# One modulation block summed on VectorE, modulation products moved behind the last sums, and low parts in another order

## The reference

```python
# first block, layer i of 2 (i = 0: differential attention, i = 1: neighbourhood attention)
sh1, sc1, g1, sh2, sc2, g2 = split(silu(c) @ ada_w[i] + ada_b[i], 6)          # for x
csh1, csc1, cg1, csh2, csc2, cg2 = split(silu(c_ctx) @ ada_w[i] + ada_b[i], 6)  # for ctx
h = rmsnorm(x, norm_mix[i]) * (1 + sc1) + sh1      # and hc from xc with csc1, csh1
x = x + g1 * attention(h, hc)                      # q, k, v = h @ wqkv, then @ wo
h2 = rmsnorm(x, norm_ffn[i]) * (1 + sc2) + sh2
x = x + g2 * conv_ffn(h2, ffn_up[i], ffn_conv[i], ffn_conv_b[i], ffn_down[i])
# ctx gets the same FFN in layer 0 only

# second block, layer l of 2
proj = rmsnorm(x, norm_g[l]) @ w_in[l]             # NSA, pool, conv, FoX, gates, merge
kc = silu(blocks(k_c) @ cmp_w1[0] + cmp_b1[0]) @ cmp_w2[0] + cmp_b2[0]   # nsa_compress, vc alike
x = x + merged_branches @ w_out[l]
```

## Time and profile before

| | us |
|---|---|
| median of 3 runs | 1631.76 (1630.92 to 1633.79) |
| the profiled execution's own time | 1631.88 |
| its span | 1629.8 |
| PE busy | 1600.1 (98%) |
| DVE busy | 930.7 (57%) |
| ACT busy | 768.1 (47%) |
| POOL busy | 548.2 (34%) |

### The profile page before, as it was taken

How to read it: one execution, slowest core, us unless ns; L and a number is a source line. 1 busy time by engine, 2 the same in 40 slices (tenths; PEclk the granted TensorE clock), 3 DMA queues, 4 the chain that set the end, 5 groups by cost and what they waited for, 6 DMA issues and landing times.

```text
span 1629.8 us, 24693 instructions
## 1 busy us (share of the span) xinstructions
PE 1600.1 (98%) x9894; PEld 1347.8 (83%) x9894; DVE 930.7 (57%) x1477; ACT 768.1 (47%) x1410; POOL 548.2 (34%) x358
## 2 busy tenths in 40 slices
PE   8999999999999999999999999999999999999998
PEld 5778557778767888879767999999999989999987
DVE  4434585555423554342265888649775567568545
ACT  5323585534313433243274755445645455454554
POOL 2224243412201222222172111026434666423554
PEclk9999999999999999999999999999999999799999
DMA  9264600443255222365314654545435544433551
GB/s 394 78 251 180 228 6 27 181 170 133 86 183 191 103 80 71 123 214 173 103 27 165 253 180 158 176 174 183 154 130 182 181 158 167 155 130 130 181 192 67
DMA packets 52465, 249.27 MB, mean 153 GB/s; under 512 B 20608, under 2 KB 20736, under 8 KB 25856
## 3 DMA queue, kind: packets, MB, share of 16 engines
q1 hardware_dynamic: 43600, 243.90, 41.9%
q10 hardware_dynamic: 8752, 3.80, 0.9%
HBM read 246.63 MB, written 1.05 MB: 152 GB/s over the span
## 4 chain that ended last, share of the span: by engine, by line
PE 89%; DVE 6%; DMA 1%; ACT 1%; issue 1%; SPq 0%; POOL 0%; POOLq 0%; ACTq 0%; DVEq 0%
PE psq L547 14%; PE psq L549 14%; PE psq L548 14%; PE psq L931 7%; PE ps L547 6%; PE ps L549 6%; PE ps L548 6%; PE psq L932 4%; PE ps L931 3%; PE ps L561 2%; PE ps L932 1%; DVE WL L529 1%; PE psq L1340 1%; PE ps L1368 1%; PE psq L2250 1%
## 5 line engine op out<-in xcount | busy, mean ns | idle before, releaser
L529 POOL TENSOR_TENSOR WL<-RAW,WH 128x1024 fp32r<-128x1024 f32 (+2 forms) x116 | 303.8, 2621 | 537.1 <-ACT WH L519 525.9
L529 DVE TENSOR_TENSOR WL<-RAW,WH 128x1024 fp32r<-128x1024 f32 (+3 forms) x264 | 325.5, 1258 | 271.8 <-ACT WH L519 271.6
L519 ACT ACTIVATE WH<-RAW 128x1024 fp32r<-128x1024 f32 (+2 forms) x380 | 361.0, 1001 | 163.2 <-DMA RAW<-wstream 115.1
L547 PE MATMUL psq<-NHL,WH 128*128 128x256 f32 (+1 forms) x1264 | 412.9, 327 | 2.6 <-DVE NHL L834 1.6
L549 PE MATMUL psq<-NHL,WL 128*128 128x256 f32 (+1 forms) x1264 | 406.8, 322 | 0.0
L548 PE MATMUL psq<-NHL,WH 128*128 128x256 f32 (+1 forms) x1264 | 406.7, 322 | 0.0
L547 PEld LDWEIGHTS psq<-NHL,WH 128*128 128x128 f32 x1264 | 241.7, 191 | 31.6 <-issue 8.7
L549 PEld LDWEIGHTS psq<-NHL,WL 128*128 128x128 f32 x1264 | 241.6, 191 | 18.0
L548 PEld LDWEIGHTS psq<-NHL,WH 128*128 128x128 f32 x1264 | 241.8, 191 | 16.8
L931 PE MATMUL psq<-NHL,WH 128*128 128x512 f32 x416 | 148.6, 400 | 0.0
L547 PE MATMUL ps<-NHL,WH 128*128 128x256 f32 (+1 forms) x368 | 122.1, 332 | 0.0
(11 more groups left out here) (388 smaller groups left out, 2877.2 us busy)
## 6 DMA issues: line engine op xcount, KB each, us to landing
RAW<-wstream SPq DMA_DIRECT2D x196, 1024.0 KB, 4.9
RAW<-wstream SPq DMA_DIRECT2D x32, 704.0 KB, 4.1
K<-first SPq DMA_DIRECT2D x4, 1024.0 KB, 16.6
X<-xin SPq DMA_DIRECT2D x2, 1024.0 KB, 6.4
V<-first SPq DMA_DIRECT2D x2, 1024.0 KB, 19.4
Q<-first SPq DMA_DIRECT2D x2, 1024.0 KB, 24.9
BR<-rpb ACTq DMA_DIRECT2D x8, 256.0 KB, 7.8
BR<-rpb SPq DMA_DIRECT2D x8, 256.0 KB, 8.3
```

The source lines that it names most:

```text
L519: e.activation(WH[:, u % 3, a:z], RAW[:, v % 3, a:z], ACT.Copy).then_inc(w_hi, 1)
L529: e.tensor_tensor(WL[:, u % 3, a:z], RAW[:, v % 3, a:z], WH[:, u % 3, a:z].bitcast(F32), ALU.subtract).then_inc(w_lo_p if pool else w_lo_v, 1)
L547: e.matmul(o, lh, rh, start=start, stop=False)
```

## The change

There are five parts.

1. The eight modulation products of block 4 leave PE. DVE multiplies each unit by its column of silu(c), one number per partition, and adds it into a new tile WSUM, 128x2048 (`dve_ada_step`: one TENSOR_SCALAR, seven SCALAR_TENSOR_TENSOR), two steps in the first down product's turn, one in each of the next six, always ahead of that turn's low parts. SP waits for these steps where it waited for PE. One product of four matmuls with a stationary of ones (`pe_ada_joint`) sums WSUM over the partitions, ahead of the second product of the second half of up; ACT's copy of the bank follows there.
2. In passage 1, PE's modulation products with units 1 and 2 of block 3 stand behind the sums of tile 7 (unit 1) and behind the spreading of the root (unit 2) instead of between the sums and ahead of the spreading. In passage 2 only one product of block 5 instead of two stands between the last sums and the root's spreading; the fourth of the block goes ahead of qkv unit 5 of layer 1.
3. In passages 1 to 3 the first tile of the first unit starts with the four matmuls that need only its high part (`pe_high_first`); the two that need its low part follow.
4. ACT copies the row of block 3 one product earlier.
5. In the head of the second block, DVE writes the low part of cmp0 between the product and the sum of KN's rotation, no longer behind the sum.

```diff
-QKV_ADA = {("qkv", 1, 4): (0, 1, 2, 3)}
+QKV_ADA = {("qkv", 1, 4): (0, 1, 2), ("qkv", 1, 5): (3,)}
+JOINT_ADA = {("up", 0, HALF_FT + 1): (7,)}
...
     for m in range(DT):
-        run_ada(4, m)
         add(("down", 0, 0, m), 2)
         add_ada(4, m)
...
         def load_unit(e, v):
-            if v >= 3 and v - 3 not in SPLIT_AT:
+            if v >= 3 and KEYS[v - 3][:2] == ("ada", 4):
+                e.wait_ge(ada_acc, KEYS[v - 3][2] + 1)
+            elif v >= 3 and v - 3 not in SPLIT_AT:
                 e.wait_ge(gemm, product(KEYS[v - 3]))
...
+        def dve_ada_step(e, k):
+            v = UNIT_OF["ada", 4, k]
+            e.wait_ge(d_raw[v % 3], 16 * (v // 3 + 1))
+            if k == 0:
+                e.tensor_scalar(WSUM[:, :], RAW[:, v % 3, :], CB[:, k, 0:1], None, ALU.mult).then_inc(ada_acc, 1)
+                return
+            e.wait_ge(ada_acc, k)
+            e.scalar_tensor_tensor(out=WSUM[:, :], in0=RAW[:, v % 3, :], scalar=CB[:, k, 0:1], in1=WSUM[:, :],
+                                   op0=ALU.mult, op1=ALU.add).then_inc(ada_acc, 1)
+
+        def pe_ada_joint(e):
+            e.wait_ge(ada_par, 3)
+            e.wait_ge(ada_acc, 8)
+            for j in range(4):
+                mm = e.matmul(AB[32 * j:32 * j + 32, :], ONE.to_broadcast([P, 32]), WSUM[:, 512 * j:512 * j + 512],
+                              start=True, stop=True)
+            mm.then_inc(gemm, 1)
...
+        def pe_high_first(e, n, key, outs, T, shared):
+            v, wh, wl = weights(key)
+            wait_weights(e, v, 0)
+            e.wait_ge(n_hi, split_base(n) + NORM_T[n] // 256)
+            for j, o in enumerate(outs):
+                w = slice(P * j, P * j + P)
+                e.matmul(o, wh[:, 0, w], NH[:, 0, 0:T], start=j == 0 or not shared, stop=False, skip_group_check=shared)
+                e.matmul(o, wl[:, 0, w], NH[:, 0, 0:T], start=False, stop=False, skip_group_check=shared)
+            pe_wait_norm(e, n, 0)
+            for j, o in enumerate(outs):
+                e.matmul(o, wh[:, 0, P * j:P * j + P], NL[:, 0, 0:T], start=False, stop=False, skip_group_check=shared)
...
             pe_sums(e, n, 6)
-            if l == 0:
-                pe_ada(e, 3, 1)
             pe_sums(e, n, 7)
-            if l == 0:
-                pe_ada(e, 3, 2)
-            else:
-                pe_ada(e, 6, 1)
+            pe_ada(e, 6 if l else 3, 1)
...
+                    if l == 0 and c == 1 and jj == 1:
+                        pe_ada_joint(e)
...
         def pe_down(e, l, c):
             for m in range(DT):
-                if l == 0 and c == 0:
-                    pe_ada(e, 4, m)
...
                 pe_ada(e, 5, 1)
-                pe_ada(e, 5, 2)
...
-                    if l == 0 and c == 0 and jj == 8:
+                    if l == 0 and c == 0 and jj == 7:
                         act_ada_row(e, 3)
+                    if l == 0 and c == 1 and jj == 1:
+                        act_ada_row(e, 4)
...
                     for half in range(1 if l == 0 else 2):
+                        if l == 0 and c == 0 and m == 0:
+                            dve_ada_step(e, 0)
+                        if l == 0 and c == 0 and m < DT - 1:
+                            dve_ada_step(e, m + 1)
                         if not (last and half):
                             split_lo(e, ahead(key), False)
...
             e.memset(CM[:, 0:384].bitcast(U32), 0).then_inc(cm_zero, 1)
-            dve_turn(e, l, 1, KN[:, :, :])
+            dve_turn_product(e, l, 1)
             lo_prep(e, l, "kf", False)
+            dve_turn_sum(e, l, 1, KN[:, :, :])
```

More of the change, by code:

```diff
@@ L228, in unit_orders @@
             add(("out", l, i), 1)
-    for name, at, b in (("up", UP_ADA, 3), ("qkv", QKV_ADA, 5), ("up", LATE_ADA, 6)):
+    for name, at, b in (("up", UP_ADA, 3), ("qkv", QKV_ADA, 5), ("up", LATE_ADA, 6), ("up", JOINT_ADA, 4)):
         for key, ks in at.items():
@@ L399, in bass_two_block_decoder @@
             HL[0] = sb("HL0", [P, HALF_FT, 512], F32R, scope)
+            WSUM = sb("WSUM", [P, 2048], F32, scope)
         with ExitStack() as scope:
@@ L465, in bass_two_block_decoder @@
         c_silu, c_zero, lam_v, lam_exp = (sem(n) for n in ("c_silu", "c_zero", "lam_v", "lam_exp"))
-        ada_row, ada_fin, ada_half, ada_par, amod = (sem(n) for n in ("ada_row", "ada_fin", "ada_half", "ada_par", "amod"))
+        ada_row, ada_fin, ada_half, ada_par, ada_acc, amod = (
+            sem(n) for n in ("ada_row", "ada_fin", "ada_half", "ada_par", "ada_acc", "amod"))
         x_res, x_low, x_sq, x_sq_v, sq_acc, sq_sum, g_pair = (
@@ L884, in pe_wide @@
             if abreast:
-                for k in range(nk):
+                for k in range(1, nk):
                     wait_weights(e, v, k)
@@ L889, in pe_wide @@
                         mm = mm3(e, o, wh[:, k, P * j:P * j + P], wl[:, k, P * j:P * j + P], xh[:, k, 0:T],
-                                 xl[:, k, 0:T], k == 0, k == nk - 1)
+                                 xl[:, k, 0:T], False, k == nk - 1)
                         if k == nk - 1:
@@ L943, in pe_both @@
             return mm
-        def pe_halves(e, key, b, wait_x):
-            pe_tiles(e, key, b, (0, 1), range(DT), NH, NL, wait_x).then_inc(gemm, 1)
         def pe_tall(e, key, banks_, n, wait_x):
@@ L987, in pe_qkv @@
                     for k in QKV_ADA.get(("qkv", 1, i), ()):
-                        if k > 2:
+                        if k > 1:
                             pe_ada(e, 5, k)
@@ L995, in pe_qkv @@
                 else:
+                    if u == 0:
+                        pe_high_first(e, n, ("qkv", l, i), [bank[b][:, :], bank[b + 1][:, :]], 512, False)
                     pe_wide(e, ("qkv", l, i), [bank[b][:, :], bank[b + 1][:, :]], 512, NH, NL, wait_x, u == 0)
@@ L1591, in pe_ffn @@
                         pe_ada_turn(e, 6)
+                    if j == 0:
+                        pe_high_first(e, 1 + 2 * l, ("up", l, j), [bank[0][:, 0:256], bank[0][:, 256:512]] if l else outs, T, l == 1)
                     if l == 1 and j == 0:
-                        pe_halves(e, ("up", l, j), bank[0], wait_x)
+                        pe_tiles(e, ("up", l, j), bank[0], (0, 1), range(1, DT), NH, NL, wait_x).then_inc(gemm, 1)
                     else:
@@ L1673, in act_ffn @@
                         act_raw_hi(e, 0, m)
-                if l == 0 and c == 0:
-                    act_ada_row(e, 4)
         def dve_gate(e, l, U):
@@ L1916, in dve_turn, with dve_turn_product @@
         def dve_turn(e, l, i, dst):
+            dve_turn_product(e, l, i)
+            dve_turn_sum(e, l, i, dst)
+        def dve_turn_product(e, l, i):
             a, s = wide2(TMP[:, 6 + 2 * i, :]), wide2(TMP[:, 7 + 2 * i, :])
@@ L1924, in dve_turn, with dve_turn_sum @@
                             ALU.mult).then_inc(nrot_v, 1)
-            e.wait_ge(nrot_v, r + 2)
+        def dve_turn_sum(e, l, i, dst):
+            s = wide2(TMP[:, 7 + 2 * i, :])
+            e.wait_ge(nrot_v, 6 * l + 3 * i + 2)
             e.wait_ge(nrot_c, 2 * l + i + 1)
```

## The result

| | us |
|---|---|
| changed kernel, 4 runs | 1614.76 median (1613.05 to 1619.34) |
| kernel before, 4 runs | 1632.24 median (1630.92 to 1633.79) |
| ratio | 0.9897, 95% interval 0.9874 to 0.9919 |
| the profiled execution | 1614.25, span 1612.1 |

What follows compares the result with a forecast made beforehand. PE was taken as the bound, busy 1600.1 of 1629.8 us. Terms -8.3 - 1.0 + 0.5 + 0.75 + 6.3 - 0.6 = -2.35 gave 1629.5 us, own range 1627 to 1632, whole range 1617 to 1635.

Steps and rivals of the forecast that it cites:

- Part 1, -8.3: First down stage: eight modulation products of 1.19 us leave PE, one joint product returns, weights still arrive: -8.3 us.
- Passage 1, -1.0 and +0.5 for the clock: Passage 1: tile 7's sums start 0.98 us earlier, -1.0; back-to-back sums may lower the clock, 0 to 1.7, taken as +0.5.
- a 0 for the copy of block 4: ACT's copy of the row and the transpose sit among up products, where ACT is half idle: 0.
- Passage 2, +0.75: Passage 2: earlier spreading -0.44, product moved into a dense stretch +1.19; sum +0.75 us, bounds -0.4 and +1.2.
- Passage 3, 0: Passage 3: PE's order is the same and the first tile doesn't wait for its low part: 0.
- Layer 0's head, +6.3: Layer 0's head: POOL gets the port first, cmp1 products +2.1 us, lower clock +4.2; bounds -0.3 and +10.1.
- The rule of the prediction: Port shared by DVE and GpSimd: whoever issues first blocks the other; 21 ns too small to count, 70 ns enough.
- Layer 1's head, -0.6: Layer 1's head: low part goes ahead of KN's sum, PE starts 0.6 us earlier, idle 1.81 instead of 2.42.
- Rival A: As forecast, but layer 1's clock doesn't fall: -8.0 us, 1621.5; chance 0.18.
- rival C: Layer 1's clock doesn't fall and DVE wins the port in layer 0 as before: 1615.2 us; chance 0.07.
- the price of a lost port in layer 0: Layer 0's head: DVE's low part stalls behind POOL's, so the products with cmp1 start 2.1 us later.

Runs made afterwards that it cites:

- the second profile of the changed kernel: Changed kernel run again with no edit, six executions: 1612.5 to 1624.2 us, median 1620.43, ratio 0.9923; the profiled execution took 1618.42.
- the three profiles with the time filled: Extra unread matmuls in PE's idle time in layer 1's head: kernel before with 20, 1625.61 us; changed kernel with 20, 1614.82; with 16, 1613.82.
- the filled changed kernel: Changed kernel with extra unread matmuls in PE's idle time in layer 1's head: 1614.82 us with 20 (5 executions), 1613.82 with 16 (4 executions).
- part 5 alone: Kernel before with only the low part of cmp0 moved ahead of KN's sum, both layers: 1629.05 us, ratio 0.9974.
- passage 1 as before: Changed kernel with passage 1's old order, modulation product 1 between the sums of tiles 6 and 7, product 2 ahead of the spreading: 1621.53 us, ratio 0.9923.
- two MEMSETs: Changed kernel with two 56-column MEMSETs on VectorE in layer 0's head, ahead of KN's rotation and of cmp1's low part: 1620.98 us, one execution.
- part 3 undone: Changed kernel with the first tile's matmuls in the old order in all three passages: 1623.77 us, one execution.
- part 4 undone: Changed kernel with ScalarE copying the row of block 3 behind up product 8 instead of 7: 1615.84 us, one execution.
- one MEMSET: Changed kernel with one 112-column MEMSET on VectorE in layer 0's head, ahead of KN's rotation: 1614.62 us, one execution.

## Why the prediction was wrong

The change was put at -2.35 and came out at -17.7 in the two profiles. Of these 15.4 us, the low clock of layer 1's head is 8.1 and layer 0's head 6.6; part 4 is 1.6 and the clock at the start 0.8, for both of which the sum had no term; passages 1 and 3 took back 0.6 and 1.1.

**Part 1, -8.3: right.** Measured -9.44 + 1.12 = -8.32, by the periods it named, and no wait for the weights.

**Passage 1, -1.0 and +0.5 for the clock: right in kind, the clock mis-sized.** Two executions of the same kernel show both terms. Where the clock stayed up (the second profile of the changed kernel):

```profile
304.98 1.95 PE L731 MATMUL ps<-ONES,TMP 128*128 128x1 f32 x16
306.85 1.06 PE L565 MATMUL ps<-RAW,CB 128*32 128x512 f32 x8
308.27 1.16 PE L801 MATMUL ps<-CONST,RS 128*128 128x128 f32 x8 [0.36 <-POOL RS L794]
...
313.72 0.50 PE L551 MATMUL psq<-NHL,WH 128*128 128x512 f32 x1 [0.83 <-POOL NHL L869]
```

From the first sums of tile 5 (303.10) it took 10.62, that is 1.08 less than before; in the first profile, with the low clock, 11.81. So the order is worth 1.1, and the clock takes 1.2 when it falls and nothing when it doesn't, where 0.5 was put. (For how long a low clock lasts, the prediction read a spacing of 0.2 from 897.4 as the clock's return; that is still the pace at 0.50, and at full clock the spacing is 0.12, from 898.0 on.)

**Part 4: left out.** The sum has a 0 for the copy of block 4 and no term for that of block 3, for which PE waited 1.4 us in the kernel before. It makes 1.6 us of the miss.

**Passage 2, +0.75: right** (-0.47 + 1.20 = +0.73). **Passage 3, 0: +1.1** (+0.30 + 0.78), because the clock fell 1.6 us behind the passage's first sums in place of 3.0 (the modulation product ahead of the spreading took 1.85 in place of 1.07), so that the spreading and all behind it came later. Up to the first tile the order there is the same, and part 3 moves nothing (above); only the clock moved. In five of the fourteen profiles, the changed kernel's second among them, it did not fall there at all. PE there, changed kernel:

```profile
883.14 1.85 PE L565 MATMUL ps<-RAW,CB 128*32 128x512 f32 x8
884.92 1.23 PE L801 MATMUL ps<-CONST,RS 128*128 128x128 f32 x4
```

**Layer 0's head, +6.3: wrong, measured -0.3** (-0.52 + 0.25), 6.6 us of the miss. The failed step is "ACT's first half is ready at 1129.53 + 1.00 = 1130.53, so the low part runs 1130.6 to 1131.8". That row of ACT writes the high part of cmp1, not of cmp0: in ACT's list the high part of cmp0 stands ahead of the four activations on the FoX logits. So nothing gated DVE's low part. It was issued while the rotation's product still ran (1121.58, in the time of the kernel before 1130.43), 0.17 earlier than put down; KN's sum was then issued 40 ns ahead of POOL in place of behind it, and VectorE's low part of cmp1 99 ns ahead (1125.91 against 1126.01). Nothing was lost. The rule of the prediction, that a lead of 70 ns gives POOL the port, stands (below); the lead was worked out from the wrong gate.

**Layer 1's head, -0.6 with the clock fallen as before: the step that failed is that the low clock would stay.** The idle time went to 1.80 as forecast (1.81), the start came 0.9 us earlier, and the clock stayed up in the profiled execution, which gave 7.8: together -8.75, 8.1 us of the miss. Rival A had named this at 0.18, and rival C, both together, at 1615.2 and a chance of 0.07, is what the first four runs hit. That it hit within 0.5 us is luck: part 4 and the start, which it left out, gave 2.4 us, and passages 1 and 3 took back 1.7. Nor is it a fixed result: of the changed kernel's ten executions five lie above 1618, and the one of them that was profiled had the fallen clock. The median of all ten is 1616.9.

What decides between fall and no fall is shown in part. Without the idle time it doesn't happen: in the three profiles with the time filled the clock stayed up, and none of the nine executions of the filled changed kernel is high. With it, it is open each time. At 1.8 us it fell in five profiles (part 5 alone, passage 1 as before, the changed kernel's second, two MEMSETs, part 3 undone) and not in three (the changed kernel's first, part 4 undone, one MEMSET); at 2.4 in all three. The odds are not the same everywhere, though: with part 5 alone, at 1.8 us, it fell in all eleven executions by their times and mean clocks (0.992 to 0.993), in the changed kernel in five of ten. What sets the odds is open. Passage 1 shows how fine the edge is. Of the nine profiles with its changed order, the clock fell where the sixteen sums began at 304.50, 304.82, 304.88 and 306.56, and stayed where they began at 304.98, 305.22, 305.26, 306.77 and 307.62. Up to there the work on PE is the same in all nine. Shifts of a tenth or two of a microsecond in the time since the program's start separate them, and the start itself moves by that much and more from one execution to the next (304.50 and 304.98 are the same program), above all with the length of the low stretch at the start. That these shifts are the cause, and not something that goes with them, was not tested. So the forecast of a single time for either passage had no ground; a mixture had. What the chip looks at there was not tested, and the price of a lost port in layer 0 stays open as well.

## What to carry to other kernels

A stretch where the clock falls after an idle time can be worth nearly as much as the work that is removed (here 6.3 to 7.9 us beside 8.3): look in every profile for stretches at 0.50, price them, and fill PE's idle time just ahead with matmuls whose result nobody reads. Here that took the high executions away. Before taking a low stretch as part of the kernel, ask how many executions show it; one profile of a kernel near the edge is one draw of several. And when a margin of 0.1 us decides a forecast, trace the semaphore of each gate to the instruction that really sets it, in the engine's own list.

## What the runs showed of the hardware

**The port of VectorE and GpSimd goes to VectorE also when it is a little late.** Where both start on operands in SBUF within 0.1 us, VectorE ran unstalled when its record began up to 42 ns behind GpSimd's (seven cases in six traces: 19, 21, 22, 22, 38, 40 and 42 ns), and was stalled for the whole of GpSimd's instruction from 47 ns on (47 to 49 ns at one place in every trace, 72, and 91 to 100 ns). The place with 49 ns in the kernel before, VectorE:

```profile
612.90 2.33 DVE L529 TENSOR_TENSOR WL<-RAW,WH 128x768 fp32r<-128x768 f32 x1
...
612.85 1.57 POOL L529 TENSOR_TENSOR WL<-RAW,WH 128x640 fp32r<-128x640 f32 x1 [5.84 <-ACT WH L519]
```

A plain low part of 768 columns takes VectorE 0.96; here it took 2.33, and GpSimd its shortest for 640 columns, 1.57. The Trainium skill ("SBUF — State Buffer", section "Who interferes with whom") gives the pair to whoever issues first; the traces agree, if one counts VectorE's record as some 45 ns earlier than it reads. Whether the record or the port is early, they can't tell.

**The clock can fall with no idle time on PE ahead of it.** In passage 1 of the changed kernel PE stood idle nowhere ahead of the fall: sixteen 128x1 sums back to back, busy 1.95, and then 0.50. It fell there in four of nine profiles; with a modulation product of 1.06 us between the two halves of the sums it fell in none of five. That points to the sums but is too few to show it.

**The step over 2048 columns.** TENSOR_SCALAR with one tensor input took 1.28, SCALAR_TENSOR_TENSOR with two 2.35.
